# Hybrid decoder step with PEER experts: 16-bit pair lookups in the selection, earlier first scores, low parts moved to VectorE, and three early gathers

## The chip, the core and the metric

The kernel runs on one core of a Trainium2 chip. The metric is the device time of one execution in microseconds. The engines are TensorE (PE, with its weight loads as PEld), VectorE (DVE), ScalarE (ACT), GpSimd (POOL) and SyncE (SP, which only issues DMAs).

## What is computed

One step of a one-layer decoder, for 1056 tokens (1024 of a prompt, 32 of eight samples) with D = 1024. After the mixer the layer adds PEER: each token picks, for each of 8 heads, 16 of 16384 single-neuron experts.

```python
q = (xb @ w_query).reshape(PEER_BLOCK, PEER_HEADS, 2, PEER_HALF)
s = jnp.einsum('bhpd,phnd->bhpn', q, sub_keys).astype(jnp.float32)
top_s, top_i = lax.top_k(s, PEER_TOPK)
cand = top_s[:, :, 0, :, None] + top_s[:, :, 1, None, :]
best_s, best_j = lax.top_k(cand.reshape(PEER_BLOCK, PEER_HEADS, PEER_TOPK * PEER_TOPK), PEER_TOPK)
e1 = jnp.take_along_axis(top_i[:, :, 0, :], best_j // PEER_TOPK, axis=-1)
e2 = jnp.take_along_axis(top_i[:, :, 1, :], best_j % PEER_TOPK, axis=-1)
eid = e1 * PEER_NKEYS + e2
gate = jax.nn.softmax(best_s, axis=-1)
act = jax.nn.gelu(jnp.einsum('bd,bhkd->bhk', xb, expert_u[eid]).astype(jnp.float32), approximate=False)
out = jnp.einsum('bhk,bhkd->bd', (gate * act).astype(xb.dtype), expert_v[eid])
```

## The kernel before

The program is written by hand, one instruction stream for each engine. Within an engine instructions run in the order of the code; semaphores order the engines among each other. Stages, in time: the mixer (up to 1217 us of the span), the selection (to 1686 us), the gate matrices (to 1932 us), a passage (to about 2036 us), and 32 groups of expert products, the first of them in the passage, with the final norm behind them.

**Two ways for the experts.** The first 320 tokens (NSP = 2 tiles of 128, and a half tile of 64) are "sparse": their expert rows are fetched by POOL's indirect DMAs (`gather`, 128 rows of 4 KB into one of five slots) and used by DVE (`sp_u`: product with the token and sum; `sp_v`: added with its weight). For the other 736 tokens all experts are computed as dense products on PE. A dense block on PE is `e_block`: 48 matmuls, three products of high and low parts. Its weight is split in two: ACT copies the high part WH (`e_split`, counted by `e_hi`), and another engine subtracts it for the low part WL (`e_low`, counted by `e_lo`). PE starts block n when `e_lo` has reached n+1, ACT splits block n+2 into the same buffer after block n. 64 blocks are computed ahead of the groups, as filler beside the selection (46) and beside the gate matrices (18).

**The selection** takes nine tiles of 128 tokens (NTILE). For each: `sel_scores` on PE (8 products of queries `qst` and KEYS into four banks), the same name on ACT (copy into `sc`), then `sel_dve` on DVE: twice 8 maxima of each of 16 score rows, 54 candidate sums of each head, 16 of them kept, then the **lookup**, which turns the 16 places of each head into the two key numbers e1 and e2 by comparing, multiplying and summing 16 by 16 tables (2048 elements a partition), then the gates and the ids. A first copy of one element (`tick`) marks the start of a tile on DVE. For tiles from the fourth on, PE transposes e1, e2 and the gates, and DVE `evict`s them into EG, one tile later. Between, PE runs SEL_E[i] blocks in tile i: FIRST_E[i] is the first of them, r counts them; the scores of the next tile come after block r = 1, and ACT's Exp of the gates after r = 2, when DVE has given `sel_b`. POOL makes all low parts of the selection and loads the queries of the next tile from DRAM, where they have been written by POOL from `qrow`. Before the first tile, `x_transposes` on PE turns the sparse tokens over, for ACT to copy.

**The gate matrices.** 92 steps: DVE builds one-hot tables (HOT, HOTG) from EG, PE multiplies them, ACT copies to `stg` and writes to DRAM (`w_dram`, counted by `w_out`, and by `w_first` where the part of the first group goes by itself).

**The passage and group 0.** SP reads back the first activations (AS) and the first gate matrix (GW), DVE multiplies them (`s_gated`) and makes low parts (AL); PE, which has computed the last two blocks of u, then waits for AL. POOL gathers for group 0 after `gw_in` has reached 64, which is the landing of all GW. DVE spreads ten `sp_u` over the dense work of group 0 (`between`), then waits for the weights (GA), and so on.

## Time and profile before

| what | value |
|---|---|
| device time, median of 3 runs | 3556.84 us (3555.5 to 3557.64) |
| time of the profiled execution | 3557.08 us |
| its span | 3554.9 us |
| TensorE busy | 3377.9 us (95%) |
| VectorE busy | 2631.3 us (74%) |
| ScalarE busy | 1013.9 us (29%) |
| GpSimd busy | 1041.2 us (29%) |
| share of the chain that ended last | PE 74%, DVE 20% |

Between the profiled time and its span lie 2.2 us. The shares are averages over the stages; what an engine is worth in a stage is read from the windows and waits of that stage.

### The profile page before, as it was taken

The page shows a single profiled execution, that of the slowest core. Times are in us where ns is not written, and L with a number is a line of the kernel's source. Part 1 is how long each engine was busy: PE and PEld are TensorE (multiplying, and loading weights), DVE is VectorE, ACT ScalarE, POOL GpSimd, SP SyncE. Part 2 cuts the span into 40 slices and gives each one's busy share as a digit, 9 for nine tenths or more (in the row PEclk, how much of TensorE's full clock was granted, in tenths as well). Part 3 has the DMA queues.
Part 4 walks back from the last instruction along what each step waited for, and adds up shares of the span by engine and source line. Part 5 has one row for each costly group of instructions (what it writes and reads, how often), then busy time and mean ns, then how long its engine had stood idle before and what let it go on. Part 6 is the DMA issues. An engine that isn't in the chain of part 4 may idle for free.

```text
span 3554.9 us, 56741 instructions
## 1 busy us (share of the span) xinstructions
PE 3377.9 (95%) x21552; PEld 3310.9 (93%) x21552; DVE 2631.3 (74%) x4906; ACT 1013.9 (29%) x1342; POOL 1041.2 (29%) x792
## 2 busy tenths in 40 slices
PE   6989999999998999997999799999999999999997
PEld 6989999799998999987998799999999999999996
DVE  5554444223444199999997999999999999999996
ACT  5742222211322233222454122222222222222222
POOL 0000000000000133232000655555555555555550
PEclk9999999999999999998999999999999999999998
DMA  2101001111322233232788999999989899989992
GB/s 107 36 34 35 35 31 63 69 41 47 127 90 72 83 114 109 100 108 78 232 270 280 358 322 329 327 338 329 323 321 330 327 335 331 324 319 332 327 324 108
DMA packets 304480, 699.00 MB, mean 197 GB/s; under 512 B 23872, under 2 KB 124224, under 8 KB 303328
## 3 DMA queue, kind: packets, MB, share of 16 engines
q0 software_dynamic: 98736, 363.50, 28.0%
q1 hardware_dynamic: 104112, 276.89, 22.3%
q10 hardware_dynamic: 101504, 56.89, 5.2%
q8 instruction: 83, 1.36, 0.2%
q14 instruction: 45, 0.37, 0.0%
HBM read 604.96 MB, written 92.22 MB: 196 GB/s over the span
## 4 chain that ended last, share of the span: by engine, by line
PE 74%; DVE 20%; DMA 2%; ACT 1%; issue 1%; DVEq 1%; ACTq 0%; SPq 0%; POOL 0%; PEldq 0%; POOLq 0%
PE PS L1484 28%; PE PS L362 16%; PE PS L1467 14%; PE PS L1187 6%; PE PS L1217 5%; DVE HOTG L1963 3%; PE PS L377 1%; DVE HOT L1959 1%; DVE HOT L1960 1%; DVE besti L1847 1%; DVE sc L1838 1%; DVE besti L1839 1%; PE PS L1407 1%; DVE pick L1895 1%; DVE best L1844 1%
## 5 line engine op out<-in xcount | busy, mean ns | idle before, releaser
L1484 PE MATMUL PS<-AH,VH 128*128 128x368 f32 x2048 | 514.1, 332 | 20.3 <-DVE AL L2064 13.2
L738 POOL DMA_INDIRECT SLOT<-rows_u,EID x256 | 349.0, 1363 | 580.3 <-DMA GW<-gate_matrices 277.0
L1484 PE MATMUL PS<-AH,VL 128*128 128x368 f32 x2048 | 514.9, 332 | 0.0
L1484 PE MATMUL PS<-AL,VH 128*128 128x368 f32 x2048 | 509.8, 330 | 0.0
L738 POOL DMA_INDIRECT SLOT<-rows_v,EID x256 | 333.9, 1304 | 202.8 <-DVE SLOT L1996 164.0
L1484 PEld LDWEIGHTS PS<-AH,VH 128*128 128x128 f32 x2048 | 365.3, 189 | 22.8 <-DVE AL L2064 14.2
L1484 PEld LDWEIGHTS PS<-AL,VH 128*128 128x128 f32 x2048 | 366.4, 189 | 0.0
L1484 PEld LDWEIGHTS PS<-AH,VL 128*128 128x128 f32 x2048 | 365.8, 188 | 0.0
L2005 DVE SCALAR_TENSOR_TENSOR XLF<-SLOT,GA,XLF 128x1024 f32<-128x1024 f32 x256 | 327.5, 1279 | 0.8 <-DMA SLOT<-rows_v,EID 0.7
L1073 ACT ACTIVATE VH<-VRAW 128x512 fp32r<-128x512 f32 x256 | 157.6, 628 | 564.0 <-PE PS L1484 564.0
L1996 DVE SCALAR_TENSOR_TENSOR SLOT<-SLOT,XHF 128x1024 f32<-128x1024 f32 x256 | 312.0, 1219 | 5.0 <-DMA SLOT<-rows_u,EID 5.0
L2076 DVE TENSOR_TENSOR HID<-HID,PS 128x736 f32<-128x736 f32 x256 | 235.7, 921 | 98.1 <-PE PS L1484 97.1
L1407 PE MATMUL PS<-XH,WH 128*128 128x368 f32 x1024 | 267.4, 340 | 21.7 <-POOL WL L710 21.7
L1407 PE MATMUL PS<-XL,WH 128*128 128x368 f32 x1024 | 263.4, 336 | 0.0
L1407 PE MATMUL PS<-XH,WL 128*128 128x368 f32 x1024 | 262.6, 336 | 0.0
L1467 PE MATMUL PS<-XH,WH 128*128 128x368 f32 x1024 | 256.1, 331 | 3.6 <-DVE WL L1977 3.6
L1467 PE MATMUL PS<-XH,WL 128*128 128x368 f32 x1024 | 257.0, 332 | 0.0
L1467 PE MATMUL PS<-XL,WH 128*128 128x368 f32 x1024 | 254.3, 329 | 0.0
L362 PE MATMUL PS<-XH,WH 128*128 128x352 f32 x984 | 219.7, 332 | 13.0 <-DVE XL L1797 5.3
L710 POOL TENSOR_TENSOR WL<-RAW,WH 128x1024 fp32r<-128x1024 f32 x47 | 130.3, 2773 | 312.0 <-ACT WH L996 312.0
L362 PE MATMUL PS<-XH,WL 128*128 128x352 f32 x984 | 214.9, 326 | 0.0
L362 PE MATMUL PS<-XL,WH 128*128 128x352 f32 x984 | 214.5, 326 | 0.0
(328 smaller groups left out, 6634.4 us busy)
## 6 DMA issues: line engine op xcount, KB each, us to landing
RAW<-experts_u SPq DMA_DIRECT2D x128, 512.0 KB, 5.8
VRAW<-experts_v SPq DMA_DIRECT2D x256, 256.0 KB, 5.7
gate_matrices<-stg ACTq DMA_DIRECT2D x22, 2048.0 KB, 9.8
GW<-gate_matrices SPq DMA_DIRECT2D x96, 384.0 KB, 6.8
RAW<-weights SPq DMA_DIRECT2D x69, 512.0 KB, 3.5
activations<-AS SPq DMA_DIRECT2D x64, 368.0 KB, 2.5
AS<-activations SPq DMA_DIRECT2D x64, 368.0 KB, 2.9
GW<-gate_matrices SPq DMA_DIRECT2D x32, 320.0 KB, 5.7
```

Source lines behind the costliest of these rows:

```text
L362: mm = pe.matmul(PS[:, 3 * s + t, 0:TH], w[:, slot, k * P:k * P + P], x[:, k - base, t * TH:t * TH + TH], start=(k == chunks[0] and n == 0 ...
L710: pool.tensor_tensor(WL[:, slot, :], RAW[:, slot, :], WH[:, slot, :].bitcast(F32), ALU.subtract).then_inc(e_lo, 1)
L738: pool.indirect_dma_start(out=SLOT[n % NSLOT][:, :], out_offset=None, in_=table, in_offset=bass.IndirectOffsetOnAxis(ap=ids, axis=0)).then ...
L1073: act.activation(VH[:, d % 2, :], VRAW[:, d % 4, :], ACT.Copy).then_inc(v_hi, 1)
L1187: ins = pe.matmul(out(h), lhs(h), rhs(h), start=start, stop=stop)
L1217: mm = pe.matmul(PS[:, 7, 0:TH], w[:, slot, k * P:k * P + P], x[:, k, t * TH:t * TH + TH], start=n == 0, stop=n == 3 * KD - 1)
L1407: mm = pe.matmul(e_bank(slot, t), w[:, slot, k * P:k * P + P], x[:, k, T0 + t * CH:T0 + t * CH + CH], start=(k == 0 and p == 0), stop=(k = ...
L1467: mm = pe.matmul(PS[:, 2 * c + t, 0:CH], w[:, c, k * P:k * P + P], x[:, k, T0 + t * CH:T0 + t * CH + CH], start=(k == 0 and p == 0), stop= ...
L1484: mm = pe.matmul(PS[:, 4 + 2 * (d % 2) + t, 0:CH], w[:, d % 2, c * P:c * P + P], x[:, c, t * CH:t * CH + CH], start=(c == 0 and n == 0), s ...
L1996: dve.scalar_tensor_tensor(out=rows, in0=rows, scalar=1.0, in1=x, op0=ALU.mult, op1=ALU.mult, accum_out=SD[:, j:j + 1]).then_inc(sp_use, 1)
L2005: dve.scalar_tensor_tensor(out=total, in0=rows, scalar=GA[:, j:j + 1], in1=total, op0=ALU.mult, op1=ALU.add).then_inc(sp_use, 1)
L2076: dve.tensor_tensor(row, row, dset(2 + d % 2), ALU.add).then_inc(acc_done, 1)
```

## The change

- **Lookup.** All operands of the lookup's tables become 16-bit floats, laid out as pairs of places: [64 pairs, 16, 2] in place of [8 heads, 16 places, 16]. The places and the table of row starts were 32-bit before. The three sums (`tensor_reduce`) become folds: four additions of halves each, of 1024, 512, 256 and 128 elements, with a drain ahead of each. `delta` and `second` are written doubled.
- **Low parts.** Of each tile's low parts POOL keeps those of r = 1, 2, 3 and starts them only when DVE has finished the tile ahead. The last block of the tile and the first of the next are made by DVE, inside the lookup: one behind the first comparison, one behind the last product. Tile 0 has 4 blocks in place of 5 and tile 7 has 5 in place of 4; their sum stays.
- **First scores.** ACT copies the queries of the first tile from PSUM into `qst` while they are computed; `sel_scores(0)` follows the transposes of one tile (not of all), and comes ahead of block 0. The other transposes come after the first block of tiles 0 and 1. The zeroing of the accumulators goes from DVE to ACT.
- **Passage.** POOL gathers rows 0 to 2 as soon as the selection is over, and the rest without waiting for GW. DVE uses these three rows (`sp_u`) before `s_gated`. SP's load of GW waits for one large write less, since the last two blocks of gate matrices write the part of group 0 by itself.

The lines of it that carry this (others renumber semaphores and allocate tiles):

```diff
-SEL_E = (5, 5, 5, 5, 5, 5, 5, 4, 5)
+SEL_E = (4, 5, 5, 5, 5, 5, 5, 5, 5)
...
             sp.wait_ge(w_out[0], 16 * (NWB // 2 + 1))
-            sp.wait_ge(w_out[1], 16 * (NWB // 2 + 1))
-            sp.wait_ge(w_first, 16)
+            sp.wait_ge(w_out[1], 16 * (NWB // 2))
+            sp.wait_ge(w_first, 32)
             for k in range(4):
                 sp.dma_start(GW[:, GWP[k]:GWP[k + 1], :, :], w_dram[0, :, GWP[k]:GWP[k + 1]]).then_inc(gw_in, 16)
+            sp.wait_ge(w_out[1], 16 * (NWB // 2 + 1))
             for s in range(4):
                 sp.dma_start(VRAW[:, s, :], v_blk[s]).then_inc(v_in[s], 16)
             sp.wait_ge(w_out[0], 16 * (NWB // 2 + 2))
...
-            for b in range(2):
-                pool.wait_ge(q_out[b], 16 * (HP // 2))
-            pool.dma_start(qst[:, :, :], q_dram[:, :, 0:P]).then_inc(qst_in, 16)
 
             def e_low(n, slot):
 
+                pool.wait_ge(e_lo, n)
                 pool.wait_ge(e_hi, n + 1)
                 pool.tensor_tensor(WL[:, slot, :], RAW[:, slot, :], WH[:, slot, :].bitcast(F32), ALU.subtract).then_inc(e_lo, 1)
...
+            e_low(0, 0)
             pool.iota(IOTA[:, :, :], pattern=[[1, NKEYS], [0, 2]], base=0, channel_multiplier=0,
                       allow_small_or_imprecise_dtypes=True).then_inc(iota_set, 1)
-            for n in range(PRE + 1):
+            for b in range(2):
+                pool.wait_ge(q_out[b], 16 * (HP // 2))
+            for n in range(1, PRE + 1):
                 e_low(n, n % 2)
             for i in range(NTILE):
+                if 0 < i <= NSP + 1:
+                    pool.wait_ge(sel_done, i + 1)
+                elif i:
+                    pool.wait_ge(sel_g, i - NSP - 1)
                 e_low(FIRST_E[i] + 1, (FIRST_E[i] + 1) % 2)
...
-                for r in range(2, SEL_E[i] + 1):
+                for r in range(2, SEL_E[i] - 1):
                     e_low(FIRST_E[i] + r, (FIRST_E[i] + r) % 2)
-            pool.wait_ge(w_mm, NSTEP + 2)
-            pool.wait_ge(gw_in, 64)
...
-            for j in range(SPR):
+            pool.wait_ge(sel_done, NTILE + 1)
+            for j in range(3):
+                gather(j, u_rows, 0, j)
+            pool.wait_ge(w_mm, NSTEP + 2)
+            for j in range(3, SPR):
                 gather(j, u_rows, 0, j)
...
+                act.activation(qst[:, j, :], PS[:, 3 * (n % 2), 0:P], ACT.Copy)
                 act.activation(thirds(qrow[:, j % 2, :]), pset(n % 2), ACT.Copy).then_inc(free_w, 1)
...
-            for b in range(NSP):
-                act.activation(xtok(b), wide(b), ACT.Copy).then_inc(tok_set, 1)
-            act.activation(XS, PS[:, 6:8, :].rearrange("p a (k t) -> p (a k) t", t=HALF), ACT.Copy).then_inc(tok_set, 1)
-            e_block(0, 0, 16)
+            act.activation(xtok(0), wide(3), ACT.Copy).then_inc(tok_set, 1)
             act.wait_ge(sel_mm, 1)
             sel_scores()
+            e_block(0, 0, 16)
...
                     e_block(n, n % 2, 16 * (n // 2 + 1))
+                    if r == 0 and i == 0:
+                        act.wait_ge(tok_mm, 2)
+                        act.activation(xtok(1), wide(0), ACT.Copy).then_inc(tok_set, 1)
+                        for b in range(NSP):
+                            act.activation(acc(b), C[:, 0:D].rearrange("p (k t) -> p k t", k=KD), ACT.Copy, scale=0.0
+                                           ).then_inc(tok_set, 1)
+                    if r == 0 and i == 1:
+                        act.wait_ge(tok_mm, 3)
+                        act.activation(XS, PS[:, 0:2, :].rearrange("p a (k t) -> p (a k) t", t=HALF), ACT.Copy
+                                       ).then_inc(tok_set, 1)
...
-                    q0 = 1 if n == NWB - 1 else 0
+                    q0 = 1 if n >= NWB - 2 else 0
...
-                pe.wait_ge(qst_in, 16 * n + 32)
+                pe.wait_ge(qst_in, 16 * n + 16)
...
-            x_transposes()
+            x_transposes(0, 6)
+            sel_scores(0)
             e_block(0, 0)
-            pe.wait_ge(tok_set, NSP + 1)
-            sel_scores(0)
+            pe.wait_ge(tok_set, 1)
             e_block(1, 1)
...
                     e_block(FIRST_E[i] + r, (FIRST_E[i] + r) % 2)
+                    if r == 0 and i == 0:
+                        pe.wait_ge(sel_sc, 1)
+                        x_transposes(1, 0)
+                    if r == 0 and i == 1:
+                        pe.wait_ge(sel_sc, 2)
+                        half_transposes()
...
                         pe.wait_ge(sel_sc, i + 1)
+                        if i < 2:
+                            pe.wait_ge(tok_set, 2 + 3 * i)
...
+            def e_low(m):
+
+                dve.wait_ge(e_lo, m)
+                dve.wait_ge(e_hi, m + 1)
+                dve.tensor_tensor(WL[:, m % 2, :], RAW[:, m % 2, :], WH[:, m % 2, :].bitcast(F32),
+                                  ALU.subtract).then_inc(e_lo, 1)
...
-                dve.tensor_copy(r(delta)[:, :, 0:1], f2[:, :, 0, 0:1])
-                dve.tensor_tensor(r(delta)[:, :, 1:TOPK], f2[:, :, 0, 1:TOPK], f2[:, :, 0, 0:TOPK - 1], ALU.subtract)
+                dve.tensor_copy(delta[:, :, 0:1, :], f2[:, :, 0, 0:1].unsqueeze(3).broadcast_to([w, HP, 1, 2]))
+                dve.tensor_tensor(delta[:, :, 1:TOPK, :], f2[:, :, 0, 1:TOPK].unsqueeze(3).broadcast_to([w, HP, TOPK - 1, 2]),
+                                  f2[:, :, 0, 0:TOPK - 1].unsqueeze(3).broadcast_to([w, HP, TOPK - 1, 2]), ALU.subtract)
+                dve.tensor_copy(second[:, :, :, :], f2[:, :, 1, :].unsqueeze(3).broadcast_to([w, HP, TOPK, 2]))
...
+                def places(x):
+
+                    return x[:, :].rearrange("p (a b) -> p a b", b=2).unsqueeze(2).broadcast_to([w, PAIRS // 2, TOPK, 2])
+
...
+                def values(x):
+
+                    return x[:, :, :, :].rearrange("p h j b -> p h (j b)").unsqueeze(2).broadcast_to([w, HP, TOPK // 2, 2 * TOPK])
+
+                def by_head(x):
+                    return x[:, :, :, :].rearrange("p (h a) j b -> p h a (j b)", h=HP)
...
+                def fold(out):
+
+                    src = pick
+                    for to in folds:
+                        dve.drain()
+                        v = src[:, :, :, :].rearrange("p a (j e) b -> p (a j) e b", e=2)
+                        dve.tensor_tensor(to[:, :, :, :].rearrange("p a j b -> p (a j) b"), v[:, :, 0, :], v[:, :, 1, :], ALU.add)
+                        src = to
+                    dve.drain()
+                    dve.tensor_tensor(out[:, :].rearrange("p (a b) -> p a b", b=2), src[:, :, 0, :], src[:, :, 1, :], ALU.add)
...
+                dve.tensor_tensor(hot[:, :, :, :], places(topf), names(startb), ALU.is_ge)
+                e_low(FIRST_E[i + 1] - 1)
                 dve.drain()
-                dve.tensor_tensor(r(pick), r(hot), over(r(delta)), ALU.mult)
+                dve.tensor_tensor(by_head(pick), by_head(hot), values(delta), ALU.mult)
+                fold(e1)
+                dve.tensor_tensor(pick[:, :, :, :], hot[:, :, :, :], names(dstart), ALU.mult)
+                fold(firstf)
                 dve.drain()
-                dve.tensor_reduce(e1v, r(pick), AX.X, ALU.add)
+                dve.tensor_tensor(topf[:, :], topf[:, :], firstf[:, :], ALU.subtract)
                 dve.drain()
-                dve.tensor_tensor(r(pick), r(hot), row(r(dstart)), ALU.mult)
+                dve.tensor_tensor(hot[:, :, :, :], places(topf), names(iota_b), ALU.is_equal)
                 dve.drain()
-                dve.tensor_reduce(e2v, r(pick), AX.X, ALU.add)
-                dve.drain()
-
-                dve.tensor_tensor(r(topf), r(topf), e2v, ALU.subtract)
-                dve.drain()
-                dve.tensor_tensor(r(hot), each(r(topf)), row(const("iota16", w)), ALU.is_equal)
-                dve.drain()
-                dve.tensor_tensor(r(pick), r(hot), over(f2[:, :, 1, :]), ALU.mult)
-                dve.drain()
-                dve.tensor_reduce(e2v, r(pick), AX.X, ALU.add)
+                dve.tensor_tensor(by_head(pick), by_head(hot), values(second), ALU.mult)
+                e_low(FIRST_E[i + 1])
+                fold(e2)
                 dve.wait_ge(sel_e, n)
                 dve.tensor_reduce(r(gsum), g3, AX.X, ALU.add)
...
-            dve.wait_ge(tok_mm, 1)
-            for b in range(NSP):
-                dve.memset(acc(b), 0.0)
...
             dve.drain().then_inc(acc_done, 2)
             u_low(1, 0)
             u_low(2, 1)
+            dve.wait_ge(tok_set, NSP + 3)
+            for j in range(3):
+                sp_u(0, j, j)
             for e in range(EARLY):
                 s_gated(0, e)
-            dve.wait_ge(tok_set, NSP + 1)
...
-                early = [0]
+                early = [3]
```

**Order on VectorE, one tile's lookup.** The names: hot is the table of comparisons, pick the products, topf the places, e and fold the sums; WL<-RAW,WH is a low part. Before:

```order
L1893 TENSOR_TENSOR hot<-topf,C 128x2048
L1895 TENSOR_TENSOR pick<-hot,delta 128x2048
L1897 TENSOR_REDUCE e_117<-pick 128x128
L1899 TENSOR_TENSOR pick<-hot,dstart 128x2048
L1901 TENSOR_REDUCE e_118<-pick 128x128
L1904 TENSOR_TENSOR topf<-topf,e_118 128x128
L1906 TENSOR_TENSOR hot<-topf,C 128x2048
L1908 TENSOR_TENSOR pick<-hot,bestf 128x2048
L1910 TENSOR_REDUCE e_118<-pick 128x128
```

and after, from the first comparison to the second sum:

```order
L1946 TENSOR_TENSOR hot<-topf,startb 128x2048
L1850 TENSOR_TENSOR WL<-RAW,WH 128x1024
L1949 TENSOR_TENSOR pick<-hot,delta 128x2048
L1941 TENSOR_TENSOR fold_115<-pick 128x1024
L1941 TENSOR_TENSOR fold_116<-fold_115 128x512
L1941 TENSOR_TENSOR fold_117<-fold_116 128x256
L1944 TENSOR_TENSOR e_122<-fold_117 128x128
L1951 TENSOR_TENSOR pick<-hot,dstart 128x2048
```

Each reduction has become four additions, and a low part stands behind the first comparison; the second one stands behind the last product (`L1958`).

**Order on ScalarE, start of the selection.** qrow are queries on their way to DRAM, XHF and XHL the turned tokens, sc the scores. Before:

```order
L990 ACTIVATE qrow<-PS 128x1056 x2
L996 ACTIVATE WH<-RAW 128x1024
L1015 ACTIVATE XHF<-PS 128x8x128 x2
L1016 ACTIVATE XHL<-PS 128x16x64
L996 ACTIVATE WH<-RAW 128x1024
L1004 ACT_TABLE_LOAD
L1004 ACTIVATE AS<-PS 128x736
L1007 ACTIVATE sc<-PS 128x2048
```

and after:

```order
L1001 ACTIVATE qst<-PS 128x128
L1002 ACTIVATE qrow<-PS 128x1056
L1008 ACTIVATE WH<-RAW 128x1024
L1026 ACTIVATE XHF<-PS 128x8x128
L1019 ACTIVATE sc<-PS 128x2048
L1008 ACTIVATE WH<-RAW 128x1024
L1016 ACT_TABLE_LOAD
L1016 ACTIVATE AS<-PS 128x736
```

The scores come ahead of the first dense block's activation, behind one copy of turned tokens in place of three.

## Rows read from the trace of the kernel before

**Rows 1.** Windows: length, busy of PE, PEld, DVE, ACT, POOL, PEclk, DMA share, GB/s
```profile
1440.00:1490.00 50.00, 46.79 (x276) 45.80 (x276) 48.04 (x220) 15.16 (x16) 15.37 (x6) 1.00 0.30 102
1760.00:1900.00 140.00, 138.07 (x1352) 128.89 (x1351) 140.00 (x224) 71.28 (x74) 0.00 (x0) 1.00 0.89 266
2200.00:3400.00 1200.00, 1200.00 (x7126) 1200.00 (x7125) 1110.37 (x1435) 290.25 (x422) 667.62 (x495) 1.00 0.91 327
```

**Rows 2.** Timeline, start of the selection: start, length, instruction, idle before, releaser
```profile
1216.79 0.48 PE L1390 MATMUL PS<-C,XH 128*128 128x128 f32 x2 [1.36 <-ACT qrow L990]
...
1224.12 0.45 PE L1396 MATMUL PS<-C,XH 128*64 128x128 f32 x4
...
1236.01 3.62 PE L1380 MATMUL PS<-KEYS,qst 128*128 128x256 f32 x16
...
1239.66 1.88 ACT L1007 ACTIVATE sc<-PS 128x2048 f32<-128x2048 f32 x1 [1.33 <-PE PS L1380]
...
1241.57 0.15 DVE L1833 COPY tick<-sc 128x1 f32<-128x1 f32 x1 [11.41 <-ACT sc L1007]
```

**Rows 3.** Timeline of DVE: starts of tiles 1, 4 and 8, and the last gates
```profile
1289.41 0.15 DVE L1833 COPY tick<-sc 128x1 f32<-128x1 f32 x1
...
1436.45 0.15 DVE L1833 COPY tick<-sc 128x1 f32<-128x1 f32 x1
...
1636.03 0.15 DVE L1833 COPY tick<-sc 128x1 f32<-128x1 f32 x1
...
1683.71 0.29 DVE L1918 TENSOR_TENSOR gate<-gate,gsum 128x128 f32<-128x128 f32 x1
```

**Rows 4.** Timeline of DVE in tile 4: first two instructions of the lookup, and its end
```profile
1467.21 2.29 DVE L1893 TENSOR_TENSOR hot<-topf,C 128x2048 bf16<-128x2048 f32 x1
1469.57 3.21 DVE L1895 TENSOR_TENSOR pick<-hot,delta 128x2048 bf16<-128x2048 bf16 x1
...
1485.46 0.28 DVE L1912 TENSOR_REDUCE gsum<-gate 128x8 f32<-128x128 f32 x1
```

**Rows 5.** Lines by themselves (ns min/median/max) and groups of DVE (mean ns)
```profile
L1895 DVE TENSOR_TENSOR pick<-hot,delta x9: 1226/3208/3264, 1272.5 to 1667.5; 128x2048 bf16<-128x2048 bf16 x9
L1852 DVE TENSOR_TENSOR cand<-best x45: 209/228/1920, 1261.3 to 1657.0; 128x64 f32<-128x64 f32 x18, 128x128 f32<-128x128 f32 x9, 128x80 f32<-128x80 f32 x9, 128x96 f32<-128x96 f32 x9
...
L1959 DVE TENSOR_TENSOR HOT<-IOTA,EG 128x1024 f16<-128x1024 f16 x81 | 55.1, 680 | 0.3 <-PEq L1440 0.3
...
L1969 DVE TENSOR_TENSOR WL<-RAW,WH 128x1024 fp32r<-128x1024 f32 x16 | 19.4, 1214 | 0.0
```

**Rows 6.** Timeline of ACT: a high part, and two block ends in a row
```profile
1466.87 1.05 ACT L996 ACTIVATE WH<-RAW 128x1024 fp32r<-128x1024 f32 x1
...
1480.17 0.79 ACT L1004 ACTIVATE AS<-PS 128x736 f32<-128x736 f32 x1 [7.75 <-PE PS L1407]
...
1488.24 0.79 ACT L1004 ACTIVATE AS<-PS 128x736 f32<-128x736 f32 x1 [6.34 <-PE PS L1407]
```

**Rows 7.** Timeline of POOL: two low parts of tile 4
```profile
1456.13 2.40 POOL L710 TENSOR_TENSOR WL<-RAW,WH 128x1024 fp32r<-128x1024 f32 x1 [11.84 <-ACT WH L996]
1467.99 3.71 POOL L710 TENSOR_TENSOR WL<-RAW,WH 128x1024 fp32r<-128x1024 f32 x1 [9.47 <-ACT WH L996]
```

**Rows 8.** Timeline, passage and group 0: what DVE and PE waited for
```profile
1949.10 1.80 DVE L1985 TENSOR_TENSOR AS<-AS,GW 128x736 f32<-128x736 f32 x2 [12.53 <-DMA GW<-gate_matrices]
...
1955.57 1.23 DVE L1996 SCALAR_TENSOR_TENSOR SLOT<-SLOT,XHF 128x1024 f32<-128x1024 f32 x1 [2.22 <-DMA SLOT<-rows_u,EID]
...
1958.51 1.23 DVE L1996 SCALAR_TENSOR_TENSOR SLOT<-SLOT,XHF 128x1024 f32<-128x1024 f32 x1 [1.09 <-DMA SLOT<-rows_u,EID]
...
1962.66 0.98 PE L1484 MATMUL PS<-AH,VH 128*128 128x368 f32 x2 [6.96 <-DVE AL L2064]
```

**Rows 9.** Windows of the passage (columns of rows 1), and a wait of SP's queue
```profile
1945.00:1950.00 5.00, 5.00 (x31) 5.00 (x30) 0.90 (x2) 0.00 (x0) 0.06 (x1) 1.00 1.05 400
...
SPq L570 <- DMA activations<-AS: 5.0, 1, 5.0
```

71 lines of the change are left out of this document (35 added, 36 removed).

## The prediction

> **What bounds the kernel now.** I read the windows by stage first, since the page's shares mix stages. In the groups of expert products TensorE is busy all the time, 1200.00 of 1200 us, with VectorE at 1110 [rows 1]; the change leaves them alone, so from the second group on the program can only be shifted. In the gate matrices VectorE is busy 140.00 of 140 us and TensorE 138: the change leaves that as well, and it starts when the last tile of the selection is evicted. So two stretches are left. In the selection, VectorE is busy 48.04 of 50 us and TensorE 46.79 [rows 1]: VectorE sets the pace, with TensorE close behind. The starts of the tiles measure it: tiles 1 to 3 last 147.0 us together (1289.41 to 1436.45), tiles 4 to 7 last 49.9 each (to 1636.03), tile 8 lasts 48.1 with its gates [rows 3]. In the passage VectorE waits for the gate matrix (12.53 us), then for gathered rows, and TensorE waits for the low part AL (6.96 us) [rows 8].
>
> **First scores.** VectorE's first tile starts at 1241.57, after all transposes, block 0, the scores and their copy [rows 2]. After: the turned tokens of one tile take half of 1216.79 to 1224.12, so 3.7; scores 3.6, their copy 1.9, gaps 0.2 [rows 2]. The new query copies on ACT (128 columns, eight of them) lie beside products, except the last, ahead of the transposes. No row shows it; it lies between 0 and the 1.05 of a copy of 1024 columns [rows 6], nearer to 0, and I take 0.3. So 1216.8 + 0.3 + 3.7 + 3.6 + 1.9 + 0.2 = 1226.5 at the latest: the start is 15.2 us earlier. The query load from DRAM, which came before it, is gone from this path.
>
> **What gives part of it back: tile 0.** VectorE now makes the low part of block 5 inside the lookup, and may do so only when ACT has split it, which is after block 3. TensorE gets there so: 1224.4 + four blocks of 8.07 (the distance of two block ends in a row [rows 6]) + 3.7 for the second transposes = 1260.4. Then ACT: activation 0.8, the scores of tile 1 (3.6) and their copy (1.9), the high part 1.05: 1267. VectorE reaches the place 30.2 us into the tile (28.6 to the lookup: 1272.5 less 2.4 less 1241.6 [rows 5], plus the new first comparison and doubled copies), at 1256.5. It stands 10.4 us, with the whole rest of the selection behind it. 15 us of lookup and gates follow, so tile 0 ends near 1282 where it ended at 1289.4: 7.5 gained. In tile 1 TensorE is still late (the half tile's transposes are there), and the same place waits some 3 us: 30 to the place, 3, and 15 behind it are 48.0. From tile 2 on 0.4 are left: ACT's Exp and its high part follow on `sel_b`, some 2.9 us, and VectorE is there after 2.5. The copies of tokens and zeros on ACT lie inside the waits of tiles 0 and 1; that they come late costs nothing else, as the gathered rows need them only in the passage.
>
> **The lookup.** Before, from the first comparison to the sum of gates: 1485.46 - 1467.21 = 18.25 us [rows 4]. That holds 3.21 for a product that takes 1.23 by itself [rows 5]; a low part on POOL began at 1467.99 and lay beside it [rows 7], and the median of nine is 3.21 as well. After: five operations on 2048 elements at 16 bits, 1.23 each by the fastest of L1895 [rows 5], 1.3 with a drain. A fold is 1024, 512, 256 and 128 elements: 0.68 for the first by the one-hot tables (1024 elements at 16 bits, 680 ns [rows 5]), then, by the line through 680 and 1226, 0.41, 0.28 and 0.21 to 0.28, with four drains 1.95 in all. Against a reduce of 2.29 and its drain that is only 0.4 less. The lookup: 6.3 for five operations + 5.8 for three folds + 0.3 for the subtraction = 12.4. Two low parts at 1.21 and one drain add 2.6, and the wait 0.4: 15.4. Doubled `delta` and `second` cost 0.45 ahead of it (256 elements, between 0.2 and 0.4 for the copy). So a lookup ends 2.4 us earlier than in tile 4.
>
> **POOL's part.** It no longer works beside the lookup, and starts again when a tile is done. Another collision may stay: in tiles 4 to 7 one addition of candidates took up to 1920 ns in place of 228 [rows 5], beside the low part at 1456.13, 19.7 us into the tile [rows 7]; tile 8 had none and was 1.8 shorter. After, this low part (r = 3) comes about 20.9 us into a tile: TensorE starts r = 0 some 2.8 ahead of the tile's start, when VectorE's second low part is there; two blocks (16.1), transposes 0.85 (as estimated from the 0.115 a matmul of rows 2), scores 3.6, their copy 1.9 and the high part 1.05 follow. The additions begin 19.7 into tile 0 (1261.3 less 1241.6 [rows 2, 5]), in tiles with an eviction some 0.7 later, and take 0.9. On the edge: none to all of five tiles, 0 to 8.5 us; I take three, 5 us.
>
> **Sum of the selection.** Tiles 1 to 3: about 48.0 + 45.9 + 44.8 = 138.7 for 147.0, so 8.3 less. Tiles 4 to 8, without collision: 45.9 each (48.1 of tile 8 less 2.4, plus 0.2 for a late gate), 229.5 for 247.6, so 18.1 less, with collisions 13.1. In all 7.5 + 8.3 + 13.1 = 28.9. What is late next is TensorE: five blocks, scores and transposes are 5 x 8.07 + 3.6 + 0.85 = 44.8 a tile, and it must wait for VectorE's two low parts. VectorE in turn waits for a block of the same tile: this ring (low part 1.2, four blocks 32.3, scores 3.6, transposes 0.85, activation and high part 1.85 [rows 6], Exp with its table estimated at 1.6) is 41.4 long, so it does not bind at full clock. Behind the selection everything moves by 28.9, as transposes and eviction of tile 8 stay.
>
> **The passage.** SP issues GW behind AS, and AS waits 5.0 us for its own write to DRAM [rows 9], so SP's shorter wait for the gate matrices gains nothing. Three products on gathered rows (3.5 us) go into the 12.53 us in which VectorE waits for GW [rows 8]. Behind GW the waits of 2.22 and 1.09 for rows go: AL, for which TensorE waits, comes 3.3 earlier. GA, behind all ten products, comes 3.3 + 3.5 + some 1.2 (waits for the last rows, an estimate) = 8 earlier, and with it the low parts of V that TensorE takes next. Against it: gathers 3 to 7 (5 x 512 KB) now run before GW has landed, where the DMA engines are at 1.05 of a full share and move 400 GB/s [rows 9]: 2.6 MB at 400 are 6.6 us, some or all of it ahead of GW. Between a gain of 8 and a loss of 3 (3.3 less 6.6) I take 4: the engines stay full through group 0, and what they really save is the three early gathers, 1.6 MB, 3.9 us. These run beside the one-hot tables with 250 us to spare.
>
> **Sum.** 28.9 + 4 = 32.9. The profiled execution took 3557.1 (its span 3554.9 and 2.2 around it), 0.2 above the median. 3557.1 - 32.9 = 3524.2; I forecast **3524 us**.
>
> **Rivals.**
>
> *The folds run at half rate.* A fold reads a pair, skips a pair, on both inputs; no row has such a pattern at 16 bits. The nearest, L1959, reads pairs again and again at 680 ns for 1024 elements. At the rate of 32-bit operations (2.29 for 2048 [rows 4]) the first three steps of a fold cost 0.53 + 0.27 + 0.13 more: 2.8 a tile, 25 in nine, of which some 3 fall into waits of tiles 0 and 1. That gives 3546; a penalty of half that size 3535. For it speaks the pattern, against it that pairs with a step of zero are fast.
> The Trainium skill, Vector Engine (DVE) Microarchitecture Reference, section 5.2, speaks for this rival: a port streams at full rate only in runs of two or more adjacent 4-byte words, and a fold has one word, then a hop. By its table (1.75 against 1.05 ns a word) I estimate 0.67 a fold, which would give about 3541. The same skill's page SBUF — State Buffer holds that two hits in one line of 16 bytes suffice, which a fold has; no row here decides between them.
>
> *Gathers delay GW in full.* The passage loses 3 in place of gaining 4: 3531. The DMA share of 1.05 speaks for it; that gathers 5 to 7 must wait for VectorE's first products speaks against all of it.
>
> *TensorE and VectorE hold each other.* The granted clock is 1.00 in the window of the selection [rows 1], though TensorE had waits in it; after, it waits twice a tile, and the clock may fall. If blocks take 9.3 us in place of 8.07, the ring is 46.3 and each tile 0.4 to 1 longer, TensorE's own 44.8 becomes 51: nine tiles cost up to 30 more, 3550. But a TensorE that is this late no longer waits, and where it was always busy its clock was 1.00 [rows 1]; so I hold this unlikely.
>
> *Slower: the 16-bit tables do not reach the double rate at all.* The products with values by head are four-dimensional, and places repeat a pair 16 times. If all five operations take 2.29 and the folds half rate, a tile costs 5 x 1.06 + 2.8 = 8.1 more, 73 in nine: 3597 less what waits hide, say 3590. It turns slower from 3.7 us a tile on, that is where half of them miss. Against it: L1895 multiplied with a repeated row and had 1226 as its fastest, and L1959 repeats pairs at 680 [rows 5].
>
> **How the numbers follow.** Forecast with its own range 3513 to 3531: 0.52. Its lower end is no collisions (5 less), a full passage (4 less) and 2 for smaller waits. Folds slower: 0.28, 3532 to 3547. GW late: 0.10. Ring: 0.05. Slower: 0.05. The range that holds 8 in 10 is 3513 to 3545. About 0.2% (7 us) is what a measurement of this kernel can tell from no change: faster 0.92, the same 0.04 (ring or half-missed rates), slower 0.04.
>
> **What would show it.** In the profile after: the first tick near 1226; L1850's first wait of some 10 us in tile 0 and near 0.4 from tile 2; 2048-element operations at 1.23 and the first fold at 0.68 (1.0 to 1.2 if the rival holds); tiles of 46 to 47.6 us; first one-hot table near 1658 in place of 1687; GW landing later than 17 us after the last step of the gate matrices if gathers delay it. Wrong would be: a tick near 1226 and yet tiles of 49, or a low part on VectorE that waits several us in every tile.

## The result, and the profile after

| | before | after |
|---|---|---|
| time, median (lowest to highest of 4) | 3557.19 us (3555.5 to 3557.64) | 3524.47 us (3523.0 to 3524.75) |
| ratio, 95% interval | | 0.9908 (0.9891 to 0.9925) |
| span of the profiled execution | 3554.9 us | 3522.8 us |
| VectorE busy, GpSimd busy | 2631.3, 1041.2 us | 2592.9, 977.9 us |

32.7 us faster, where 32.9 were forecast. First the page of the kernel after: its section 1 (busy time by engine) and the chain that ended last.

```profile
PE 3372.2 (96%) x21552; PEld 3306.5 (94%) x21552; DVE 2592.9 (74%) x5013; ACT 1017.0 (29%) x1352; POOL 977.9 (28%) x773
...
PE 76%; DVE 17%; DVEq 2%; ACT 2%; DMA 1%; issue 1%; ACTq 0%; SPq 0%; PEldq 0%
```

The timeline of VectorE after: the starts of tiles 0, 1, 4 and 8 and the last gates, which answer to [rows 3]; and the first low part that VectorE makes itself, in tile 0.

```profile
1228.68 0.15 DVE L1871 COPY tick<-sc 128x1 f32<-128x1 f32 x1 [30.30 <-ACT sc L1019]
...
1269.03 1.23 DVE L1850 TENSOR_TENSOR WL<-RAW,WH 128x1024 fp32r<-128x1024 f32 x1 [10.22 <-ACT WH L1008]
...
1283.84 0.15 DVE L1871 COPY tick<-sc 128x1 f32<-128x1 f32 x1
...
1423.15 0.15 DVE L1871 COPY tick<-sc 128x1 f32<-128x1 f32 x1
...
1609.06 0.15 DVE L1871 COPY tick<-sc 128x1 f32<-128x1 f32 x1
...
1654.20 0.29 DVE L1968 TENSOR_TENSOR gate<-gate,gsum 128x128 f32<-128x128 f32 x1
```

The gates end at 1654.49 us in place of 1684.00: 29.5 us, of the 32.1 that the span lost. The starts of tiles 1 to 8 stand 46.5 us apart on the mean ((1609.06 - 1283.84) / 7), where it was 49.5 [rows 3]. The first start is only 12.9 us earlier, since this execution was 2.7 us later before the change begins. ScalarE's last copy of queries, before and after:

```profile
1215.52 1.05 ACT L990 ACTIVATE qrow<-PS 128x1056 f32<-128x1056 f32 x1 [10.60 <-PE PS L362]
...
1218.18 1.04 ACT L1002 ACTIVATE qrow<-PS 128x1056 f32<-128x1056 f32 x1
```

The code of the stages ahead is the same but for the copies into `qst`, of which the last puts this one off by 0.17 us. Over the fourteen profiled executions of this document the moment lies anywhere from 1215.2 to 1218.6 us, with the changed code too, so from here on stretches are compared and not clock times. Counted from this copy, the last gates end 32.2 us earlier, not 29.5 (468.5 us behind it before, 436.3 after).

Groups of VectorE after, in the selection (busy us, mean ns of one | idle before): the 16-bit products, the first step of the folds, the other steps, the cast of the keys, the additions of candidates.

```profile
L1949 DVE TENSOR_TENSOR pick<-hot,delta 128x2048 f16<-128x2048 f16 x9 | 11.0, 1226 | 0.8
...
L1941 DVE TENSOR_TENSOR fold<-pick 128x1024 f16<-128x1024 f16 x27 | 18.7, 693 | 2.2
...
L1941 DVE TENSOR_TENSOR fold<-fold 128x512 f16<-128x512 f16 (+1 forms) x54 | 19.4, 359 | 4.0
...
L1895 DVE CAST bestf<-besti 128x256 f16<-128x256 uint32 x9 | 8.9, 991 | 0.7
...
L1890 DVE TENSOR_TENSOR cand<-best 128x64 f32<-128x64 f32 (+3 forms) x45 | 7.8, 241 | 0.0
```

Every product takes 1226 ns, and a fold of pair, skip, pair runs at the rate of pairs in a row: 693 ns for 1024 elements, where rows of before had 680 for the one-hot tables [rows 5]. The additions of candidates, up to 1920 ns before [rows 5], are never held any more (held: standing still until GpSimd's operation beside them has ended); the cast right behind them now is. Timeline of tile 5, GpSimd and VectorE:

```profile
1489.71 2.40 POOL L713 TENSOR_TENSOR WL<-RAW,WH 128x1024 fp32r<-128x1024 f32 x1 [10.81 <-ACT WH L1008]
...
1489.79 2.47 DVE L1895 CAST bestf<-besti 128x256 f16<-128x256 uint32 x1
```

In tiles 3, 5 and 7 it takes 2.33 to 2.47 us in place of 0.29: 6.3 us in all. Windows after, from the last query copy to the start of tile 4, and from there to the first one-hot table (columns as in [rows 1]):

```profile
1218.20:1423.10 204.90, 201.23 (x1227) 198.05 (x1227) 171.54 (x913) 66.56 (x69) 40.75 (x20) 0.99 0.32 109
1423.10:1657.50 234.40, 221.95 (x1291) 218.36 (x1290) 220.32 (x1159) 65.33 (x69) 39.62 (x19) 0.98 0.32 106
```

The first window is TensorE's (201 of 205 us, VectorE has 33 us of gaps), in the second it has gaps of 12.5. These do not lie everywhere, as the windows of tiles 4, 5 and 8 show:

```profile
1423.15:1468.53 45.38, 45.38 (x267) 44.97 (x266) 43.10 (x231) 13.43 (x14) 8.01 (x5) 0.99 0.28 94
1468.53:1516.31 47.78, 45.70 (x261) 44.85 (x260) 45.18 (x232) 13.41 (x14) 8.04 (x5) 0.96 0.36 124
...
1609.06:1654.49 45.43, 38.67 (x231) 38.06 (x229) 43.00 (x231) 11.65 (x13) 7.18 (x3) 0.98 0.30 101
```

TensorE has no gap in tile 4, 2.1 us in tile 5 with its held cast, and 6.8 in the last tile. The passage after: VectorE's wait for the gate matrix, and TensorE's next waits.

```profile
1923.99 1.76 DVE L2032 TENSOR_TENSOR AS<-AS,GW 128x736 f32<-128x736 f32 x2 [13.59 <-DMA GW<-gate_matrices]
...
1928.30 0.98 PE L1515 MATMUL PS<-AH,VH 128*128 128x368 f32 x2 [4.65 <-DVE VL L2036]
...
1934.01 0.60 PE L1515 MATMUL PS<-AH,VH 128*128 128x368 f32 x2 [1.66 <-DVE AL L2113]
...
1941.40 0.98 PE L1515 MATMUL PS<-AH,VH 128*128 128x368 f32 x2 [4.09 <-DVE AL L2113]
```

The product with GW comes 25.1 us earlier than in [rows 8], though the stage ahead ends 29.6 earlier: GW is 4.5 us late. Still the passage gains: from the first one-hot table to a wait of TensorE for AL that both kernels have it is 343.2 us in place of 346.4. That wait, before and after:

```profile
2033.42 0.60 PE L1484 MATMUL PS<-AH,VH 128*128 128x368 f32 x2 [3.74 <-DVE AL L2064]
...
2000.71 0.73 PE L1515 MATMUL PS<-AH,VH 128*128 128x368 f32 x2 [3.79 <-DVE AL L2113]
```

This stretch scatters: over the nine profiled kernels below that have the changed passage word for word it is 342.5 to 345.2 us, 343.8 on the mean. The old passage (346.4 here, 347.3 in p2 below) lies above all nine, so the gain is real, some 3 us, and single differences under 2.7 us in it say nothing.

### The profile page after: what moved, and what is told of

It is laid out like the page before. It is cut to its first block, busy times and chain, and to the rows that moved or that the text cites. A ratio compares the mean times of both kernels' runs of the same rounds, so it can differ in the third digit from the quotient of the medians.

```text
span 3522.8 us, 56958 instructions
## 1 busy us (share of the span) xinstructions
PE 3372.2 (96%) x21552; PEld 3306.5 (94%) x21552; DVE 2592.9 (74%) x5013; ACT 1017.0 (29%) x1352; POOL 977.9 (28%) x773
## 4 chain that ended last, share of the span: by engine, by line
PE 76%; DVE 17%; DVEq 2%; ACT 2%; DMA 1%; issue 1%; ACTq 0%; SPq 0%; PEldq 0%
PE PS L1515 28%; PE PS L366 16%; PE PS L1498 14%; PE PS L1207 6%; PE PS L1237 5%; DVE HOTG L2013 3%; PE PS L1430 2%; DVE HOT L2009 1%; PE PS L381 1%; DVE HOT L2010 1%; DVE fold L1941 1%; DVE besti L1885 1%; DVE sc L1876 1%; DVE besti L1877 1%; DVEq L1939 1%
## 5 line engine op out<-in xcount | busy, mean ns | idle before, releaser
L745 POOL DMA_INDIRECT SLOT<-rows_u,EID x256 | 347.3, 1357 | 578.6 <-DVE XLF L2052 257.6
L745 POOL DMA_INDIRECT SLOT<-rows_v,EID x256 | 334.1, 1305 | 203.1 <-DVE SLOT L2043 164.7
L366 PE MATMUL PS<-XH,WH 128*128 128x352 f32 x984 | 221.1, 334 | 13.1 <-DVE XL L1828 5.3
L1430 PEld LDWEIGHTS PS<-XH,WH 128*128 128x128 f32 x1024 | 182.2, 189 | 11.1 <-DVE WL L1850 10.2
```

Source lines behind the costliest of these rows:

```text
L366: mm = pe.matmul(PS[:, 3 * s + t, 0:TH], w[:, slot, k * P:k * P + P], x[:, k - base, t * TH:t * TH + TH], start=(k == chunks[0] and n == 0 ...
L745: pool.indirect_dma_start(out=SLOT[n % NSLOT][:, :], out_offset=None, in_=table, in_offset=bass.IndirectOffsetOnAxis(ap=ids, axis=0)).then ...
L1430: mm = pe.matmul(e_bank(slot, t), w[:, slot, k * P:k * P + P], x[:, k, T0 + t * CH:T0 + t * CH + CH], start=(k == 0 and p == 0), stop=(k = ...
```

## The experiments

All are edits of the changed kernel. The table has the stretch from the last query copy to the start of tile 4, that from there to the end of the last gates, that from the copy to the first one-hot table, and the times.

| kernel | copy to tile 4 | tile 4 to gates | copy to one-hot | median us | ratio to before |
|---|---|---|---|---|---|
| before | 220.9 | 247.6 | 471.5 | 3557.2 | 1 |
| after | 205.0 | 231.3 | 439.4 | 3524.5 | 0.9908 |
| u1, new lookup only | 204.7 | 251.3 | 459.0 | 3544.2 | 0.9963 (0.9949 to 0.9978) |
| u2, moved low parts only | 214.6 | 246.4 | 464.1 | 3549.2 | 0.9976 (0.9967 to 0.9986) |
| u4, neither | 208.0 | 247.8 | 458.9 | 3541.3 | 0.9962 (0.9948 to 0.9976) |
| u5, neither, scores late | 212.5 | 245.9 | 461.4 | 3546.7 | 0.9972 (0.9962 to 0.9981) |
| u3, scores late | 205.0 | 231.3 | 439.4 | 3525.1 | 0.9905 (0.9888 to 0.9921) |
| m1, tile 0 on GpSimd | 205.3 | 231.1 | 439.4 | 3525.3 | 0.9912 (0.9895 to 0.9929) |
| s1, a block to the last tile | 196.8 | 234.9 | 435.8 | 3523.8 | 0.9910 (0.9893 to 0.9926) |
| c1, cast first | 203.0 | 227.0 | 433.1 | 3520.2 | 0.9900 (0.9883 to 0.9916) |
| p1, GW behind three gathers | 205.0 | 231.4 | 439.4 | 3522.9 | 0.9901 (0.9884 to 0.9917) |
| p2, passage of before | 205.0 | 231.3 | 439.3 | 3527.2 | 0.9916 (0.9899 to 0.9932) |
| k2, c1 and p1 | 203.1 | 226.9 | 433.1 | 3518.2 | 0.9889 (0.9872 to 0.9905) |
| k1, c1, p1 and s1 | 194.9 | 233.5 | 430.7 | 3512.6 | 0.9873 (0.9857 to 0.9890) |

**The low parts back on GpSimd.** The two `e_low` calls in VectorE's lookup go, and:

```diff
-                if 0 < i <= NSP + 1:
-                    pool.wait_ge(sel_done, i + 1)
-                elif i:
-                    pool.wait_ge(sel_g, i - NSP - 1)
                 e_low(FIRST_E[i] + 1, (FIRST_E[i] + 1) % 2)
...
-                for r in range(2, SEL_E[i] - 1):
+                for r in range(2, SEL_E[i] + 1):
```

> The changed kernel with one part undone: the two low parts of each tile that VectorE took over (L1850) are back on GpSimd, with its two waits for the selection gone. My account (the low parts are worth little, since TensorE was busy for nearly the whole of tiles 1 to 8): VectorE's wait of 10.2 us in tile 0 and of 3.7 us in tile 1 goes, but the same blocks of first scores still have to pass TensorE, so tile 0 ends at most some 4 us earlier; against it two more GpSimd low parts a tile run beside VectorE's 16-bit passes and hold some of them back by about 2 us each. Together 3521 to 3532 us, most likely 3526. Rival, that moving the low parts is a main source of the gain: 8 x 1.5 us come back in the lookup and the selection, 3536 us or more. Rival, that the move cost time by the stall in tile 0: 3514 to 3517 us.

3544.2 us: my account (3521 to 3532) was wrong, the rival with 3536 or more right. Timeline of tile 5 in this kernel, GpSimd and then VectorE:

```profile
1505.25 2.98 POOL L713 TENSOR_TENSOR WL<-RAW,WH 128x1024 fp32r<-128x1024 f32 x1 [9.54 <-ACT WH L1004]
1509.69 2.62 POOL L713 TENSOR_TENSOR WL<-RAW,WH 128x1024 fp32r<-128x1024 f32 x1 [1.46 <-ACT WH L1004]
...
1506.10 3.22 DVE L1944 TENSOR_TENSOR pick<-hot,delta 128x2048 f16<-128x2048 f16 x1
...
1510.15 2.81 DVE L1937 TENSOR_TENSOR fold<-fold 128x512 f16<-128x512 f16 x2
```

The product that takes 1.23 us ends 1.1 us after the low part beside it has ended: it did not run slower, it stood still. The hold goes the other way too: the first low part was issued while the comparison ahead of the product had 0.77 us left to run, and took 2.98 us in place of 2.40. In [rows 7] one met a comparison [rows 4] with 1.51 us left and took 3.71. The two fold steps (0.79 by themselves) end 0.65 after theirs. With a candidate addition and one more fold, tile 5 is held four times, some 7.8 us, where the changed kernel pays one held cast (2.2) and two low parts of its own (2.4). Over the selection the means of this kernel's lines carry the same: 2786 ns for this product, 1209 for the first fold step. All 20 us lie behind the start of tile 4; ahead of it the kernel is no later (204.7 against 205.0): there TensorE, which has no gap in its tiles 0 to 3, sets the pace.

**The old lookup, low parts on VectorE.** Its core (the other tables alike):

```diff
-                dve.tensor_tensor(by_head(pick), by_head(hot), values(delta), ALU.mult)
-                fold(e1)
+                dve.tensor_tensor(r(pick), r(hot), over(r(delta)), ALU.mult)
+                dve.drain()
+                dve.tensor_reduce(e1v, r(pick), AX.X, ALU.add)
```

> The changed kernel with the lookup of the kernel before put back in its place (32-bit and bf16 tables, two reduces in the place of the eight folds); the two low parts stay on VectorE, the early first scores and the passage stay too. My account (the selection is bound by VectorE in tiles 1 to 8, and the lookup went from 18.25 to about 12.8 us without the low parts): about 3 us a tile come back, 8 x 3 = 24 us, so 3546 us, range 3540 to 3552; the duration of the products and reduces is 3208 and 3264 ns again, and TensorE's busy share of the selection falls. Rival, that TensorE and not VectorE set the length of the tiles by now (it was busy 144.7 of 147.1 us in tiles 1 to 3): a slower lookup would show only where TensorE runs dry, so 3530 to 3538 us.

3549.2: inside my range of 3540 to 3552, and 24.7 over the changed kernel, as the 24 of the difference in length had it. One part of my account was wrong: the products do not take 3208 ns again but 1226, as nothing of GpSimd's lies beside them. The two windows answer to those of after above:

```profile
1218.30:1432.90 214.60, 204.47 (x1235) 200.47 (x1236) 186.46 (x873) 66.55 (x69) 41.52 (x20) 0.98 0.30 104
1432.90:1682.30 249.40, 225.66 (x1283) 221.26 (x1281) 238.81 (x1109) 65.33 (x69) 40.05 (x19) 0.95 0.29 100
```

TensorE now has gaps from the start on (204 of 215). No run has the 16-bit comparisons with the reductions kept, so how the 3.1 us a tile divide is an estimate from durations: two comparisons from 2.29 to 1.23 are 2.1, three folds of 1.84 to 1.94 us (tile 4) in place of reductions of 2.20 to 2.36, with their drains, some 1.3, and the doubled tables take 0.4 back.

**Neither of the two.** Both edits together.

> The changed kernel with both parts of the lookup undone at once: the tables and reduces of the kernel before, and all low parts on GpSimd; the early first scores and the passage stay. It closes a square with the two runs that undo one part each (3544.2 us with the new lookup alone, 3549.2 us with the moved low parts alone) and the changed kernel itself (3524.5 us). My account after these: 3557.8 less about 3.5 us for the passage and the start, so 3554 us, range 3551 to 3557; then the new lookup alone is worth some 10 us, the moved low parts alone some 5 us, and both together some 29.5 us, twice their sum, since a 16-bit pass that runs beside a GpSimd low part waits until that is done. Rival, that the parts simply add: 3544.2 + 3549.2 - 3524.5 = 3569 us.

3541.3, below my range of 3551 to 3557 and far below the rival's 3569, and below both kernels that have one of the two parts. So by stretches the new lookup alone gives nothing (459.0 against 458.9), the moved low parts alone cost 5.2 us, and both together give 19.5. Why the new lookup gains nothing with the low parts on GpSimd is seen in the groups of VectorE in this kernel:

```profile
L1927 DVE TENSOR_TENSOR pick<-hot,delta 128x2048 bf16<-128x2048 bf16 x9 | 25.0, 2773 | 0.7
L1925 DVE TENSOR_TENSOR hot<-topf,C 128x2048 bf16<-128x2048 f32 x9 | 22.8, 2535 | 0.7
L1929 DVE TENSOR_REDUCE e<-pick 128x128 f32<-128x2048 bf16 x9 | 20.6, 2286 | 0.7
```

Products and comparisons are held, the reduce never is: 2286 ns in every kernel that has it. More than a third of the old lookup is out of GpSimd's reach; in the new one the folds have taken its place, and they are held like any operation on two tensors. By the excess of the means over the free durations, u1 loses 47 us in its lookups and u4 21; the difference is about what the shorter lookup saves where nothing is held (24.7, u2 against the changed kernel). The Trainium skill, page SBUF — State Buffer, section "Who interferes with whom", says the same of two inputs: an operation of VectorE on two SBUF tensors contends with GpSimd's reads for the whole instruction, `tensor_reduce` never does. These traces agree, with 1.6 to 2.3 us for most hits by a low part of 2.4, and less where an operation met only its end.

**Late scores.** On TensorE, and alike on ScalarE:

```diff
             x_transposes(0, 6)
-            sel_scores(0)
             e_block(0, 0)
+            sel_scores(0)
```

> The changed kernel with the first scores of the selection again behind block 0 of the steps' scores, on TensorE and on ScalarE. My account, formed on the changed trace: tile 0's search starts 10 to 13 us later, but VectorE waited 10.2 us in tile 0 for ScalarE's block of weights, which came from TensorE, and that block now comes 4 us earlier or at the same time; TensorE has no gap in tile 0 either way. So the stall shrinks by what the start is late, and the time is the same within 2 us: 3523 to 3527 us. Rival, the one of the prediction, in which the early scores are worth their lead less the stall: 8 us come back, 3531 to 3534 us.

3525.1, and the stretches are the same to a tenth: as my account had it. The starts of tiles 0 and 1 on VectorE:

```profile
1237.26 0.15 DVE L1871 COPY tick<-sc 128x1 f32<-128x1 f32 x1 [38.48 <-ACT sc L1019]
...
1284.29 0.15 DVE L1871 COPY tick<-sc 128x1 f32<-128x1 f32 x1
```

Tile 0 starts 18.7 us after the last query copy in place of 10.5, and tile 1 at 65.7 as in the changed kernel. The 8.2 us had only been waiting time at the low part. The edit takes back the order alone; the split transposes stay early.

> The kernel with neither the new lookup nor the moved low parts (3541.3 us), and now also with the first scores of the selection behind block 0 again; only the passage is left of the change. The same edit beside the moved low parts moved nothing (3525.1 against 3524.5 us, the stretch from the last query copy to the first one-hot 439.4 us in both). My account: what makes it worth nothing there is the wait of VectorE for ScalarE's weights in tile 0, which doesn't exist with the low parts on GpSimd; so here the late scores cost their whole delay, 10 to 13 us: 3552 to 3555 us, and the stretch goes from 458.9 to 469 to 472 us. Rival: early scores are worth nothing anywhere, and the 12.7 us by which the stretch of the kernel with neither is shorter than that of the kernel before come from elsewhere: 3541 us.

Neither account fits: 3546.7, +5.4 us by medians (the runs of the two kernels nearly meet: 3545.6 is u4's highest, 3545.5 the lowest here), 2.6 by the stretch, where I had 10 to 13. The start of tile 0 is 8.2 us later, but tile 0 then lasts 47.9 in place of 51.8, as one operation of it is held and not three. In the kernel with early scores these were (VectorE, in tile 0):

```profile
1256.71 3.26 DVE L1927 TENSOR_TENSOR pick<-hot,delta 128x2048 bf16<-128x2048 bf16 x1
...
1266.43 4.33 DVE L1937 TENSOR_TENSOR hot<-topf,C 128x2048 bf16<-128x2048 f32 x1
...
1274.97 2.37 DVE L1961 TENSOR_TENSOR GATES<-gate,gsum 128x128 f32<-128x128 f32 x1
```

So a shift also shuffles which operation meets a low part. Of the 10.1 us between this kernel and before, 7.4 are at the start of tile 0 (18.7 after the query copy, not 26.1), with most transposes behind it and the queries no longer loaded from DRAM; the rest I did not take apart.

**Tile 0's low parts on GpSimd, the others on VectorE.** `if i:` ahead of both calls in the lookup, `if 1 < i` and `elif i > 1` in GpSimd's waits, and its loop in tile 0 runs to the last block.

> The changed kernel with the two low parts of tile 0 alone back on GpSimd; those of tiles 1 to 7 stay on VectorE. Tile 0 then has no stall of 10.2 us, and took 49.1 us with all low parts on GpSimd against 55.2 us. My account: TensorE had no gap from 1241.6 to 1286.4 us, so VectorE only runs ahead of it by 6 us; of this the tile 1 low parts take back 4 to 6 us as a longer wait for ScalarE's weights (3.7 us before), and the time is 3522 to 3525 us. Rival: the later tiles are bound by VectorE, and 6 us ahead in tile 0 stay 6 us ahead at the end: 3518 us.

3525.3, a hair over my range (3522 to 3525) and far from the rival's 3518. Tile 0 lasts 49.2 us in place of 55.2, and tile 1 waits:

```profile
1315.75 1.23 DVE L1850 TENSOR_TENSOR WL<-RAW,WH 128x1024 fp32r<-128x1024 f32 x1 [8.17 <-ACT WH L1008]
```

8.2 us in place of 3.7. Tile 2 starts 113.9 us after the query copy in both kernels: the stall of tile 0 cost nothing. Tile 4 starts at 205.3, not 205.0; between the two this kernel has its held cast in tile 2 and the other in tile 3, and later in tiles 4 and 6 in place of 5 and 7.

**A block of TensorE moved out of the first stretch.**

```diff
-SEL_E = (4, 5, 5, 5, 5, 5, 5, 5, 5)
+SEL_E = (3, 5, 5, 5, 5, 5, 5, 5, 6)
```

> The changed kernel with one block of first scores fewer in tile 0 (three) and one more in the last tile (six). VectorE's first low part in tile 0 is then that of one block earlier, so its stall of 10.2 us goes for the most part (to 0 to 2 us), and every later low part comes one block earlier against TensorE, so the 3.7 us in tile 1 go too; in the last tile TensorE has one block more, of some 8.5 us, beside the gaps that it had there. My account: the same as with the low parts of tile 0 on GpSimd where TensorE is the bound up to tile 4, but here TensorE's work itself is moved to the tiles in which it had 13 us of gaps: 3518 us, range 3516 to 3522. Rival: the sixth block of the last tile ends after the last gates and holds up the next stage by most of its length: 3526 to 3530 us.

3523.8 us: above my range (3516 to 3522) and below the rival's (3526 to 3530), so neither account fits. The first stretch falls by 8.2 us, one block of 8.07 [rows 6]: that is what it means that TensorE sets the pace there. The second grows by 3.5, with a new wait in the last tile:

```profile
1631.89 1.22 DVE L1850 TENSOR_TENSOR WL<-RAW,WH 128x1024 fp32r<-128x1024 f32 x1 [3.16 <-ACT WH L1008]
```

3.6 us are left at the first one-hot table. The median (3523.8) shows 0.7; its lowest run, the profiled one, took 3517.9, three others 3523.3 to 3524.4. The profiled one lies 6.6 us under that of the changed kernel: 3.6 of the stretch, and 3.0 because its query copy came that much earlier (1215.2). By itself the gain is not shown by times.

**The cast ahead of the low part.** The semaphore is one that an earlier stage had left at NQ.

```diff
+                    if r == 3:
+                        pool.wait_ge(hist_set, NQ + i + 1)
                     e_low(FIRST_E[i] + r, (FIRST_E[i] + r) % 2)
...
-                dve.tensor_copy(r(bestf), r(besti))
+                dve.tensor_copy(r(bestf), r(besti)).then_inc(hist_set, 1)
```

> One wait added to the changed kernel: GpSimd's low part of a tile's fourth block starts only after VectorE's cast of the candidates' keys (L1895), which in tiles 3, 5 and 7 took 2.33 to 2.47 us in the place of 0.29 us while that low part ran. My account: the low part starts at most 0.9 us later, its wait costs TensorE nothing, and the three stretched casts give back 3 x 2.1 us: about 3518 us, range 3517 to 3521. Rival: since the low part started in the last microsecond before or after the cast in six of eight tiles, the shift lets it fall on the reads or on TensorE's need, and the time stays at 3524 us.

3520.2, in my range (3517 to 3521); the stretch is 6.3 us shorter, exactly the three held casts. Tile 5, GpSimd and VectorE:

```profile
1485.68 2.40 POOL L713 TENSOR_TENSOR WL<-RAW,WH 128x1024 fp32r<-128x1024 f32 x1 [11.82 <-DVE bestf L1897]
...
1485.31 0.29 DVE L1897 CAST bestf<-besti 128x256 f16<-128x256 uint32 x1
```

The low part starts 0.4 us behind the cast, beside maxima, which are not held.

**The passage.** First GW's wait put back behind three gathers:

```diff
             pool.wait_ge(w_mm, NSTEP + 2)
+            pool.wait_ge(gw_in, 64)
             for j in range(3, SPR):
                 gather(j, u_rows, 0, j)
```

> The changed kernel with GpSimd's wait for the gate weights' load put back behind the three early gathers, so that only those three run ahead of that load and the other gathers of the first step follow it. In the changed trace ScalarE read the gate weights 25.1 us before its time in the kernel before, while the stage ahead ended 29.6 us earlier: 4.5 us lost to the gathers that share the queues. If the two gathers issued at 8 to 12 us after the stage's end are what delays the load, it comes 2 to 4.5 us sooner and the time is 3520 to 3523 us. Rival: gathers 3 and 4 then land later than the step's first matmuls want them, and what the load gives is taken back there: 3524 to 3528 us. Rival: the three early gathers alone delay the load, and nothing changes: 3524.5 us.

```profile
1919.18 1.76 DVE L2033 TENSOR_TENSOR AS<-AS,GW 128x736 f32<-128x736 f32 x2 [8.83 <-DMA GW<-gate_matrices]
...
1932.70 0.98 PE L1516 MATMUL PS<-AH,VH 128*128 128x368 f32 x2 [6.92 <-DVE AL L2114]
```

GW is read 4.8 us sooner, so the gathers were what delayed it; but the rows come later, TensorE waits 6.9 us for AL, and at the common wait for AL 0.7 us are left, less than that stretch scatters. The median (3522.9) lies in the range of my account, but is only 1.6 lower, too little to tell it from the rivals. Then the whole passage as before:

> The changed kernel with the whole passage between the two last stages as it was in the kernel before: no gather ahead of the gate weights' load, the late order of the loads on SyncE's queue. My account, from the two traces: the passage as changed gave 3.1 us (TensorE's 3.8 us wait for AL moved from 349.7 to 346.6 us after the first one-hot), so 3527.6 us, range 3526 to 3530, with the gate weights read 4.5 us sooner after the stage's end and the gathers for the low half 3 to 8 us later. Rival: the early gathers only trade places with the gate weights, and the time is the same, 3523 to 3525 us.

3527.2 (3524.2 to 3529.1): near my 3527.6 and over the rival's 3523 to 3525, though the lowest run lies in there; its passage to the common wait is 347.3 us, where the kernels with the changed passage have 342.5 to 345.2.

**Together.** The edits of the sections above.

> Two of the edits together: GpSimd's fourth low part behind the cast of the keys, and the gate weights' wait behind the three early gathers. The one gave 4.3 us by medians and took 6.3 us off the stretch from the last query copy to the first one-hot, the other gave 1.6 us by medians and 0.7 us in the trace; they touch different stages, so they add: 3518 us, range 3516 to 3520.

> The same two edits and the block moved from tile 0 to the last tile, which alone took 3.6 us off the stretch from the last query copy to the first one-hot, though its median was only 0.7 us under the changed kernel's. My account: with the casts no longer stretched the later tiles are 45.1 us and leave TensorE less room for the sixth block of the last tile, so 0 to 3.6 us of its gain remain on top: 3516 us, range 3513 to 3520. Rival: the block of 8.5 us in the last tile is then in full behind the last gates, and the time is 3520 to 3524 us, over that of the two edits without it.

3518.2, in my range, and 3512.6 (3510.9 to 3514.6), just below the 3513 to 3520 that I had, and far from the rival: the second is faster than all the others, 11.9 us under the changed one, and its runs do not meet that one's. The first stretch is 10.0 us shorter and the second 2.1 longer, with 6.4 us of waiting in the last tile:

```profile
1630.09 1.23 DVE L1853 TENSOR_TENSOR WL<-RAW,WH 128x1024 fp32r<-128x1024 f32 x1 [6.41 <-ACT WH L1011]
```

The trace's stretches account for 8.7 us of the 11.9. The moved block alone had shown 0.7 by medians, here it shows 5.6 (to k2). The two profiled executions, 6.1 us apart, say what that is made of: 2.3 are the stretch, 1.9 the earlier query copy (1216.5, not 1218.4) and 2.3 the passage, whose code is the same in both (342.7 and 345.1); the groups behind it take 0.4 back. So the block is worth some 2.3 there, within my 0 to 3.6, and the rest is scatter; for the unprofiled runs it stays open.

## Why the prediction was right

| term | forecast | measured |
|---|---|---|
| start of tile 0 after the last query copy | 15.2 earlier | 15.5 earlier (10.5, not 26.05) |
| start of tile 1, likewise | 7.5 earlier | 8.2 earlier |
| VectorE's wait in tile 0, tile 1, later tiles | 10.4, 3, 0.4 each | 10.2, 3.7, none |
| tiles 1 to 3 | 138.7 | 139.3 |
| products, first fold step | 1.23, 0.68 | 1.226, 0.693 |
| held operations | 3, 5 us, additions, in tiles 4 to 8 | 3, 6.3 us, cast, tiles 3, 5 and 7 |
| tile 4 to the last gates | 13.1 less | 16.2 less |
| selection in all | 28.9 less | 32.2 less (29.5 by the clock) |
| passage | 4 less | 3.2 less |
| stages ahead, not changed | 0 | 2.7 more in the profiled execution |

**The total was in part luck.** The mechanisms are the ones that were forecast, but the sum was not as exact as 32.9 against 32.7 looks. Between the profiled executions the selection gave 3.3 us more than forecast and the passage 0.8 less; against that stood 2.7 us by which the changed kernel's execution was late before the change begins. That the three cancel was luck. With the selection as it was, the sum would have been 36.2 and the forecast 3521.

**The first scores** and the query copies came as worked out; the forecast clock time of 1226.5 for the first tick missed by 2.2, because of the same 2.7 us. With the last `qst` copy I had added 0.3 us; it took 0.17.

**The lookup** ran as sized, with the folds at the full rate of pairs: the likeliest rival, folds at half rate, fell, as the 693 ns show. With it fell, for pairs that skip a pair, the rule of the Trainium skill's Vector Engine (DVE) Microarchitecture Reference, section 5.2 (full rate only in runs of adjacent words; its rows are of 32-bit streams). The 16-byte lines of the Trainium skill's page SBUF — State Buffer, section "Specifications (TRN2)" (two hits in a line suffice), agree with the 693 ns.

**The step that was off** is the time of tiles 4 to 8, and in it first the collision term. I had it at the edge of the additions; by the time it comes, these are over and the cast stands there. It cost 6.3 and not 5, of which 4.3 in tiles 4 to 8, and one hit fell into tile 3. These tiles were 3.1 us better than forecast: 0.8 for a hit less in them, and some 0.5 us a tile, as they last 45.4 without one and I had put 45.9. That is the wait of 0.4 that did not come: from the first comparison to the sum of gates tile 4 takes 14.9 us, where I had 15.4.

```profile
1452.66 1.23 DVE L1946 TENSOR_TENSOR hot<-topf,startb 128x2048 f16<-128x2048 f16 x1
...
1467.52 0.28 DVE L1962 TENSOR_REDUCE gsum<-gate 128x8 f32<-128x128 f32 x1
```

**What the sum hid.** The total holds only with all parts in place; the experiments show that its terms are not what the parts are worth. The 15.2 us of the start end in a wait, and 8.2 of them (the scores ahead of block 0) bring nothing in this kernel. I wrote that VectorE's stall in tile 0 leaves "the whole rest of the selection behind it", and that what is late next is TensorE; m1 and s1 show that up to tile 2 TensorE already was the bound, so the stall was free, and a block less of TensorE's work was worth its whole 8.2 there. In tile 3 VectorE counts again: without its held cast the first stretch is 2.0 us shorter (c1). And I booked the two low parts as a cost of 2.6 a tile against one held product, while the same low parts left on GpSimd hold three operations of the new lookup in each of tiles 4 to 7 (u1), where the old one had one held: nothing of the shorter lookup is left then.

**The passage**: the gathers delayed GW by 4.5 of the 6.6 us that I had as the most, and the gain of 3.2 is near the 4 taken. TensorE's granted clock stayed (0.99 and 0.98 in the two windows above, 0.98 and 0.95 over the same stretches before), so the rival of the two engines holding each other never came up.

## What to carry to other kernels

Before an operation on VectorE is made faster, look at what GpSimd does beside it: a reduce can be replaced by folds of the same or less length and lose all of it again, unless the other engine's work is moved at the same time. Judge each part of a change by the stretch in which it acts and by the engine that has no gaps there; a wait of 10 us on the engine with 33 us of gaps cost nothing, and work moved off the other was worth its full length in that stretch, of which 4.5 us (s1) and 5.8 us (k1 against k2) went back in the last tile. Compare stretches of the traces before you compare times: a total that comes out as forecast can hide two errors and the scatter of stages that were not touched. Where a held operation shows as a maximum far above its median, one wait in the right place takes it away (6.3 us here for a wait of 0.4).

## What the runs showed of the hardware

- A GpSimd low part of 2.4 us stops VectorE's products, comparisons, folds, the additions of candidates and the cast (0.29 to 2.47 us), while reduces (2286 ns in every kernel that has them), maxima and searches (276 to 288 ns on the mean in each) ran beside it unchanged. It goes the other way as well: a low part issued beside a running comparison took 3.7 us in place of 2.4 [rows 7]. That the cast of 256 elements is held I had not expected.
- Folds that read a pair and skip a pair on both inputs take 693 ns for 1024 elements of 16 bits; operations of that size without the skip take 680 to 692.
- The same code ahead of the selection ended between 1215.2 and 1218.6 us in fourteen profiled executions, and the same passage took 342.5 to 345.2 us in nine, so a difference of some 3 us between two spans says nothing about an edit.
